# Order of the six split-precision matmul passes over two PSUM banks in the MLPs of a two-layer decoder step

## The reference

```
def sqrelu_mlp(h, w1, w2):
    return jnp.square(jax.nn.relu(h @ w1)) @ w2

def residual_layer(y, mod, n1, n2, mixer, w1, w2):
    ...
    h = modulate(rms_norm(y, n2), mod[3], mod[4])
    y = y + (mod[5] * sqrelu_mlp(h, w1, w2)).astype(y.dtype)
    return y, state
```

## Time and profile before

| | us |
|---|---|
| median of 3 runs (lowest, highest) | 2392.49 (2391.9, 2393.16) |
| span of the profiled execution, first to last instruction | 2391.7 |
| the same with what lies around it, taken as the median of the runs | 2392.49 |
| TensorE matmul busy | 2199.4 (92% of the span) |
| TensorE weight load busy (beside the matmuls) | 1664.8 (70%) |
| VectorE busy | 820.6 (34%) |
| ScalarE busy | 450.4 (19%) |
| MLP of layer 0, about 907.9 to 1315.0 | 407.1 |
| MLP of layer 1, about 1955.0 to 2362.0 | 407.0 |

### The profile page before, as it was taken

The page is one execution under the profiler, slowest core; times in us unless marked ns, Lnnn a source line. Parts: engine busy times, 40 slices in busy tenths (PEclk is TensorE's granted clock), DMA queues, the critical chain, the costliest instruction groups (busy, mean ns, idle before and its releaser), DMA issues.

```text
span 2391.7 us, 27972 instructions
## 1 busy us (share of the span) xinstructions
PE 2199.4 (92%) x11961; PEld 1664.8 (70%) x11961; DVE 820.6 (34%) x1564; ACT 450.4 (19%) x754; POOL 81.5 (3%) x143
## 2 busy tenths in 40 slices
PE   4889999989999888999999679998888979999997
PEld 2554444667788548999999235545776559999996
DVE  3002122125411336454553226012323445545352
ACT  2122001014432113111111341011001121111111
POOL 2000001310010000000000000000000000000000
PEclk8889999859976798999999879996555989999999
DMA  9435212320031311222223651010112212222221
GB/s 321 170 141 227 85 48 71 107 71 1 19 106 36 106 36 53 87 72 88 88 82 128 248 209 39 32 35 3 38 38 90 71 32 75 88 88 78 80 70 40
DMA packets 128143, 209.06 MB, mean 87 GB/s; under 512 B 6487, under 2 KB 72942, under 8 KB 127870
## 3 DMA queue, kind: packets, MB, share of 16 engines
q1 hardware_dynamic: 115742, 163.88, 20.5%
q0 software_dynamic: 12320, 44.05, 5.3%
HBM read 194.94 MB, written 17.04 MB: 89 GB/s over the span
## 4 chain that ended last, share of the span: by engine, by line
PE 88%; DVE 5%; DMA 3%; ACT 2%; SPq 1%; issue 1%; DVEq 0%; ACTq 0%
PE ps L1116 11%; PE ps L1114 11%; PE ps L1113 11%; PE ps L876 10%; PE ps L1082 5%; PE ps L1158 5%; DMA wring<-in_ada_w 3%; PE ps L1043 3%; PE ps L1155 3%; PE ps L807 2%; PE ps L956 2%; PE ps L1195 2%; PE ps L942 2%; PE ps L1209 1%; PE ps L779 1%; PE ps L1210 1%
## 5 line engine op out<-in xcount | busy, mean ns | idle before, releaser
L1113 PE MATMUL ps<-arena_r,wring_r 128*128 128x288 f32 x2048 | 570.3, 293 | 35.0 <-DVE hT_r L1900 35.0
L1116 PE MATMUL ps<-arena_r,wring_r 128*128 128x288 f32 x2048 | 439.8, 296 | 0.0
L1113 PEld LDWEIGHTS ps<-arena_r,wring_r 128*128 128x128 f32 x2048 | 386.4, 189 | 35.3 <-issue 17.7
L1116 PEld LDWEIGHTS ps<-arena_r,wring_r 128*128 128x128 f32 x2048 | 328.6, 189 | 0.0
L1114 PE MATMUL ps<-hT_r,wring_r 128*128 128x288 f32 x1024 | 286.5, 295 | 0.0
L1114 PE MATMUL ps<-arena_r,wring_r 128*128 128x288 f32 x1024 | 284.5, 294 | 0.0
L876 PE MATMUL ps<-wring,hT 128*128 128x512 f32 (+1 forms) x560 | 247.9, 597 | 4.1 <-ACT hT L1292 4.1
L1472 ACT ACTIVATE wring_r<-wring 128x2048 fp32r<-128x2048 f32 x64 | 122.4, 1916 | 627.8 <-DMA wring<-in_mlp_w 627.8
L1114 PEld LDWEIGHTS ps<-hT_r,wring_r 128*128 128x128 f32 x1024 | 194.2, 190 | 0.0
L1114 PEld LDWEIGHTS ps<-arena_r,wring_r 128*128 128x128 f32 x1024 | 192.4, 188 | 0.0
L876 PEld LDWEIGHTS ps<-wring,hT 128*128 128x128 f32 (+1 forms) x560 | 98.8, 181 | 133.1 <-issue 132.9
(11 more groups left out here) (331 smaller groups left out, 2589.5 us busy)
## 6 DMA issues: line engine op xcount, KB each, us to landing
wring<-in_mlp_w SPq DMA_DIRECT2D x64, 1024.0 KB, 5.6
wring<-in_ada_w SPq DMA_DIRECT2D x24, 2048.0 KB, 17.1
wring<-in_even_w_in SPq DMA_DIRECT2D x7, 2048.0 KB, 8.1
wring<-in_gla_w_in SPq DMA_DIRECT2D x6, 2048.0 KB, 17.7
arena<-in_cache_cmp_kv POOLq DMA_DIRECT2D x16, 256.0 KB, 10.0
arena<-in_cmp_w POOLq DMA_DIRECT2D x2, 2048.0 KB, 27.5
wring<-in_cache_diff_k POOLq DMA_DIRECT2D x16, 256.0 KB, 3.1
wring<-in_cache_diff_v POOLq DMA_DIRECT2D x16, 256.0 KB, 4.1
```

The source lines that it names most:

```text
L1113: pe.matmul(bank, hi, x_hi[:, k, cols], start=k == 0, stop=False)
L1116: mm = pe.matmul(bank, lo, x_hi[:, k, cols], start=False, stop=k == KC - 1)
```

## The change

The pass with the rest of the activations gets a loop of its own over the two banks. In a slice the order of banks was first, first, second, second, first, second; it becomes first, second, first, second, first, second. The number of instructions, the order of the six weight operands (four times high, twice rest), the waits and the semaphores stay. Within each bank the order of accumulation is the same as before.

More of the change, by code:

```diff
@@ L1113, in mlp @@
                                     pe.matmul(bank, hi, x_hi[:, k, cols], start=k == 0, stop=False)
+                                for bank, cols in zip(banks, halves):
                                     pe.matmul(bank, hi, x_lo[:, k, cols], start=False, stop=False)
```

## The result

The changed kernel takes 2403.45 us (median of 4, 2402.22 to 2406.52) against 2392.82 (2391.9 to 2394.01): 10.6 us slower, ratio 1.0054 with a 95% interval of 1.0038 to 1.0070. My forecast was 2392.5 with a range of 2388 to 2398, so it missed.

What follows compares the result with a forecast made beforehand. The prediction took TensorE's matmul-to-matmul pace in the MLPs to bound the kernel. With a switch priced like a repeat, 2392.5 + 0 = 2392.5 us, range 2388 to 2398.

Steps and rivals of the forecast that it cites:

- What bounds the kernel: In both MLP stretches, 407 us each, nothing but TensorE's own pace from matmul to matmul sets the time.
- The change costs 2048 x (s - r): In the MLPs, 2048 gaps turn from same-bank repeat (price r) into bank switch (price s); everything else follows from these prices.
- s - r to be 0: In MLP slices, a bank switch was taken to cost the same as a repeat, so the change adds 0 us.
- Stream and load are both just under the gap, and both stay as they are: MLP gap of 0.1316 us taken as set by column stream (0.12) and weight load (0.115), both unchanged.
- The upper bound of 6.8 us: Most the MLPs could lose: s - r of 0.0033 us, read from gaps inside a slice, times 2048.
- rival 2: In the MLPs a repeat costs more than a switch: 23.8 us less, or 71 if neighbours are delayed too; chance 0.09.
- Rival 1: In every MLP slice a switch costs more than a repeat: 5.7 us more, 2398.2 us; chance 0.14.
- Rival 3: The clock falls to half in the MLPs: 666 us more, 3058 us; chance 0.01.

Runs made afterwards that it cites:

- e3: Changed kernel's bank order with the moving operands in the order of the kernel before, some products in the wrong bank; 2397.9 us, one execution.
- e5: The kernel before, unchanged, run and profiled again; 2393.07 us, ratio 0.9998.
- e14: The kernel of e3, new banks with old moving order, timed over twelve runs against the kernel before; 2394.59 us, ratio 1.0017.
- e2: Bank order of the kernel before with the changed kernel's moving operands, some products in the wrong bank; 2389.2 us, one execution.
- e6: The changed kernel, unchanged, run and profiled again; 2403.91 us, ratio 1.0038.
- e13: The kernel of e2, old banks with new moving order, timed over twelve runs against the kernel before; 2402.65 us, ratio 1.0034.
- e17: The changed kernel with high weights in the third pass too, so all six loads of a slice read the same block; 2392.71 us, one execution.
- e9: Kernel before's bank order, with the same weights and moving operand in all six matmuls of a slice; 2392.91 us, one execution.
- e10: Changed kernel's bank order, with the same weights and moving operand in all six matmuls of a slice; 2394.70 us, one execution.
- e11: The kernel before with 224 columns instead of 288 in slices 1 to 7 of each chunk; 2284.92 us.
- e12: The changed kernel with 224 columns instead of 288 in slices 1 to 7 of each chunk; 2287.93 us.
- e15: The kernel before's order with 384 columns instead of 288 in every matmul, the halves overlapping; 2649.23 us.
- e1: Against the kernel before, a slice's banks go first, first, second, second, second, first, operands staying with their own bank; 2404.4 us, ratio 1.0052.
- e4: Against the kernel before, a whole chunk is done on the first bank, then on the second, weights high, high, rest; 2402.28 us, ratio 1.0042.
- e18: Against the kernel before, three passes on the first bank, then three on the second, weights and moving operands reordered, products correct; 2406.62 us, ratio 1.0031.
- e7: The kernel before with one more wait per chunk, TensorE waiting for the end of its own last matmul; 2441.61 us.

## Why the prediction was wrong

**What bounds the kernel: right.** TensorE's pace in the MLPs is the whole question. The two stretches grew by 5.2 and 5.7 us of busy time (0.9 of it the later rise of the clock) and no wait appeared.

**"The change costs 2048 x (s - r)", everything by bank: wrong, and the first step that failed.** I wrote that everything follows from the price of a repeat against that of a switch. The edit also changes the order in which the moving operands come: high 1, rest 1, high 2, rest 2 became high 1, high 2, rest 1, rest 2. I checked that the six weight operands kept their order and that every matmul kept its 288 columns, and did not ask the same of the operand that streams. Over the profiles, the old moving order showed 0.79 in seven stretches and 0.78 in one (before, e3, e5, e14), the new one 0.80 in eight and 0.78 in two (after, e2, e6, e13, e17), whichever banks they had.

**"s - r to be 0": right for what it says.** With equal operands the two bank orders differ by nothing (e9, e10), and e14 is not told from the kernel before. But the small differences inside a slice, from which I worked out s - r, are no prices of a repeat or a switch. In the changed kernel one gap of 0.140 us stands at every fourth matmul and the others are 0.130 to 0.132; a slice has six, so the long gap falls now on one pass and now on another.

**"Stream and load are both just under the gap, and both stay as they are": the second step that failed.** The gap is neither of them. The floor of a narrow matmul, most likely the load's, is 0.111 (e11, e12), the stream's 0.120 (half of the 0.240 at half clock), and the gap is the stream with 0.010 to 0.013 on top; with 384 columns 0.013 on top (e15). This remainder differs between orders: 0.0100, 0.0116 or 0.0133 (a sixth of 0.78, 0.79 and 0.80, less 0.120). I saw 0.0116 of it unexplained, named it under rival 2, and still took the pace for fixed by two causes that did not explain it.

**The upper bound of 6.8 us: too low.** It took the spread of gaps inside a slice of the kernel before for the most that a reordering could do. The spread inside is no bound on the mean: the new order has another pattern of gaps, with another sum. What the rows did show was that 0.0116 x 6144 = 71 us had no explanation, and no row bounded it from above.

**The rivals.** Rival 1 had the right sign and half the size (5.7 against 10.6) with the wrong mechanism: e1 and e4, slow with four and more repeats, and e9 against e10 refute a price of a bank switch. Rival 2, a repeat that costs, is refuted by the result itself, which has no repeats and is slower, and by e9 against e10. Rival 3 did not come: the granted clock is 1.00 in every stretch of 300 us shown above. The Trainium skill (TensorE: Matmul & The Clock Gate, "A second HAM failure mode: psum-queue depth-cycling") tells of a kernel that cycled through banks, idled between its groups and kept falling back to half clock. Six bank switches in a slice, without idle time, left the clock at 1.00 here. For the gap the Trainium skill (TensorE: Matmul & The Clock Gate, "Back-to-back issue gap") gives columns / 2.4 + 2.5 ns for a lone stream, so 122.5 ns at 288 columns and 162.5 at 384. The traces have 131.6 and 173.3, 9 and 11 ns more; no run showed that the loads make the difference.

**What stays open.** The cause inside the chip. Shown is that the mean gap takes few values; that the usual value goes with the order of the moving operands and not with the banks (e13, e14); that two MLPs of one execution can differ; and that it can change with the half that is streamed (e4). Not shown is why, nor which property of the order counts: old and new order differ both in how high and rest take turns and in how the halves do. The starts in the traces, read to the nanosecond, give one hint. In all eight stretches in which the new moving order runs at 0.80, the long gap of 0.139 to 0.140 us comes back every fourth matmul, without an exception, whatever the banks (after, e2, e6, e13, e17). In e1 and e18, also at 0.80, no gap is over 0.135 at full clock, so one pace can be made up in more than one way. Single runs of the kernel before at 2402 us and more also have no profile behind them.

## What to carry to other kernels

When an edit reorders matmuls, list what each gap has on both sides before and after: bank, weights and moving operand. I did it for two of three, and the third made the difference. To tell them apart, cross them, as e13 and e14 do, even where the products are then of no use. Where TensorE runs without a wait, compare the pace by the count of matmuls in a fixed stretch at full clock, for each stretch on its own, since a single stretch can show a pace that is not the usual one. A mean can also hide two paces, as in e4; then compare shorter pieces.

## What the runs showed of the hardware that I had not expected

- Back-to-back float32r matmuls at full clock cost 0.010 to 0.013 us each over their columns (288: 0.130 to 0.133 against 0.120; 384: 0.173 against 0.160), at half clock nothing that shows (0.240 and 0.320, which is columns / 1.2 GHz).
- The pace of a long run of such matmuls takes few values, 0.78, 0.79 or 0.80 us for six (once in a while 0.807, e7), and can hold one for 500 slices; the same instructions can run at 0.78 in one MLP and 0.80 in the other (e2, e17). In e4 it is 0.79 on the first half of the columns and 0.80 on the second, in every chunk at full clock.
- In the changed kernel one gap in four is 0.140 us and the rest are 0.130 to 0.132; the place of the long one moves through the slice of six.
- Two bank orders with the same six operands ran at the same pace, 2280 or 2281 matmuls in 300 us (e9, e10).
- With 224 columns the gap is 0.111 at full clock and 0.213 at half clock, more than the columns and the remainder explain, and there the order of operands makes less than 0.001 us a slice.
